# Expert weights of a routed block fetched in 4 KB pieces, with the contraction rows renumbered to match

## What is computed

```python
def hierarchical_moe(x, wg, bg, we, be, w_gate, w_up, w_down):
    ...
    g_logits = (xt @ wg + bg).astype(jnp.float32)
    ...
    e_logits = (xt @ we + be).astype(jnp.float32).reshape(-1, N_GROUPS, EXPERTS_PER_GROUP)
    ...
    for e in range(N_EXPERTS):
        h = jax.nn.silu(xt @ w_gate[e]) * (xt @ w_up[e])
        y = y + combine[:, e:e + 1] * (h @ w_down[e])
```

## Time and profile before

| What | Value |
|---|---|
| Median of 3 runs | 832.91 us (832.02 to 835.53) |
| Profiled execution, own time | 830.33 us |
| Its span | 828.3 us |
| TensorE (PE) busy | 766.8 us, 93% of the span |
| VectorE / ScalarE / GpSimd busy | 489.6 / 448.2 / 216.9 us |
| Moved by DMA | 186.75 MB |
| Chain that ended last | PE 78%, DVE 8%, ACT 5% of the span |

### The profile page before, as it was taken

How to read it: one execution, slowest core, us unless ns; L and a number is a source line. 1 busy time by engine, 2 the same in 40 slices (tenths; PEclk the granted TensorE clock), 3 DMA queues, 4 the chain that set the end, 5 groups by cost and what they waited for, 6 DMA issues and landing times.

```text
span 828.3 us, 10555 instructions
## 1 busy us (share of the span) xinstructions
PE 766.8 (93%) x3635; PEld 632.3 (76%) x3635; DVE 489.6 (59%) x639; ACT 448.2 (54%) x572; POOL 216.9 (26%) x126
## 2 busy tenths in 40 slices
PE   4999999999999999999999957999999999999960
PEld 3887878888788888888888855787888888787850
DVE  7704566576643213013122366888989898998965
ACT  6244666565733322223212315788888888888832
POOL 5555332323233444444435034000000000000013
PEclk9999999999999999999999959999999999999995
DMA  8664562521221352333348258999999999957945
GB/s 308 187 232 153 194 224 76 205 77 56 72 77 52 113 192 84 95 102 101 102 142 320 79 176 335 404 408 410 409 410 409 409 409 407 401 227 264 344 151 203
DMA packets 126631, 186.75 MB, mean 225 GB/s; under 512 B 9148, under 2 KB 61956, under 8 KB 126596
## 3 DMA queue, kind: packets, MB, share of 16 engines
q1 hardware_dynamic: 119156, 167.82, 56.2%
q10 hardware_dynamic: 5136, 10.08, 3.2%
q0 software_dynamic: 2304, 8.39, 2.8%
HBM read 158.99 MB, written 27.28 MB: 225 GB/s over the span
## 4 chain that ended last, share of the span: by engine, by line
PE 78%; DVE 8%; ACT 5%; issue 3%; POOL 2%; DMA 2%; ACTq 1%; POOLq 0%; DVEq 0%; SPq 0%
PE ps L974 24%; PE ps L976 23%; PE ps L975 23%; PE ps L1199 2%; DVE w_lo L371 1%; PE ps L1037 1%; PE ps L1063 1%; PE ps L1147 1%; ACT w_hi L360 1%; PE ps L1206 1%; DMA x<-in_x 1%; POOL slots L613 1%; PE ps L1048 1%; DMA raw_mg<-slots,slot_idx 1%; ACT xn L906 1%
## 5 line engine op out<-in xcount | busy, mean ns | idle before, releaser
L365 POOL TENSOR_TENSOR w_lo<-raw,w_hi 128x1024 fp32r<-128x1024 f32 x72 | 175.0, 2434 | 256.2 <-ACT w_hi L353 256.2
L353 ACT ACTIVATE w_hi<-raw 128x1024 fp32r<-128x1024 f32 x73 | 76.9, 1058 | 183.8 <-PE ps L976 174.1
L974 PE MATMUL ps<-xn_hi,w_hi 128*128 128x512 f32 x352 | 141.9, 403 | 0.0
L976 PE MATMUL ps<-xn_hi,w_lo 128*128 128x512 f32 x352 | 137.4, 390 | 0.0
L975 PE MATMUL ps<-xn_lo,w_hi 128*128 128x512 f32 x352 | 137.2, 390 | 0.0
L974 PE MATMUL ps<-w_hi,xT_hi 128*128 128x512 f32 x256 | 103.2, 403 | 10.8 <-DVE xT_lo L1708 5.4
L976 PE MATMUL ps<-w_hi,xT_lo 128*128 128x512 f32 x256 | 100.1, 391 | 0.0
L975 PE MATMUL ps<-w_lo,xT_hi 128*128 128x512 f32 x256 | 100.0, 390 | 0.0
L640 POOL DMA_INDIRECT raw_mg<-slots,slot_idx x7 | 6.8, 978 | 297.0 <-ACTq L957 288.7
L975 PEld LDWEIGHTS ps<-xn_lo,w_hi 128*128 128x128 f32 x352 | 66.2, 188 | 15.1 <-issue 1.9
L974 PEld LDWEIGHTS ps<-xn_hi,w_hi 128*128 128x128 f32 x352 | 66.2, 188 | 14.9 <-issue 1.9
(11 more groups left out here) (279 smaller groups left out, 1437.9 us busy)
## 6 DMA issues: line engine op xcount, KB each, us to landing
raw<-in_w_in SPq DMA_DIRECT2D x52, 512.0 KB, 3.7
raw_mg<-in_exp_w_down SPq DMA_DIRECT2D x36, 512.0 KB, 8.3
raw<-in_exp_w_gate SPq DMA_DIRECT2D x28, 512.0 KB, 9.9
raw_a<-in_exp_w_gate SPq DMA_DIRECT2D x27, 512.0 KB, 9.8
raw_c<-in_exp_w_up SPq DMA_DIRECT2D x27, 512.0 KB, 8.8
slots<-raw SPq DMA_DIRECT2D x24, 512.0 KB, 6.5
raw_mg<-in_exp_w_up SPq DMA_DIRECT2D x21, 512.0 KB, 9.2
raw<-in_exp_w_up SPq DMA_DIRECT2D x16, 512.0 KB, 9.2
```

What stands on the lines that cost most here:

```text
L353: nc.scalar.activation(w_hi[:, b % HI_SLOTS, :], raw_buf(b), ACT.Copy)\
L365: eng.tensor_tensor(w_lo[:, b % HI_SLOTS, :], raw_buf(b), w_hi[:, b % HI_SLOTS, :].bitcast(F32), ALU.subtract)\
L974: pe.matmul(dst, hi_l, hi_r, start=start, stop=False)
L976: return pe.matmul(dst, lo_l, hi_r, start=False, stop=stop)
```

## The change

It changes which bytes a block holds, and with that which rows of the contraction stand on which partition.

- **Gate and up blocks.** Row 8p + k of the weights goes to partition p, group k. A block is two neighbouring k, so each partition reads one piece of 4 KB, and neighbouring partitions' pieces start 16 KB apart.
- **Down blocks.** A block is 128 full rows of 1024 columns: one piece of 4 KB a partition, the block being one run of 512 KB. It holds one contraction group for both halves of the output, so TensorE fills three matmuls into bank 5 and three into bank 6, block after block (`down_block`).
- **Rows written in that order.** VectorE writes `xn2` permuted: column 8j + k goes to place k * 128 + j. It reads `x_rows` and `g2_rows` with a step of 8 floats (32 bytes) and writes without gaps. Everything that reads `xn2` (transposes, scatter, tile 0) is unchanged.
- **Router weights.** They are read in the same numbering. The pieces that land in SBUF stay 16 and 64 bytes.

```diff
+        def by_eighths(rows):
+
+            return rows.rearrange("p (j k) -> p k j", k=KD)
...
             def load_block(places, r, src):
                 bufs, sems = places
-                sp.dma_start(bufs[r].rearrange("p (k n) -> p k n", k=2), src).then_inc(sems[r], 16)
+                sp.dma_start(bufs[r], src).then_inc(sems[r], 16)
 
             def tile_source(e, before, r):
 
-                if r < 4:
-                    return rows2(w_g[e], 2 * r, 0)
                 if r < 8:
-                    return rows2(w_u[e], 2 * (r - 4), 0)
-                return rows2(w_d[before], 2 * (r % 2), 512 * ((r - 8) // 2))
+                    w = (w_g, w_u)[r // 4][e]
+                    return w.rearrange("(p k) n -> p (k n)", k=KD)[:, 2 * (r % 4) * DE:2 * (r % 4 + 1) * DE]
+                return w_d[before][(r - 8) * P:(r - 7) * P, :]
...
-                    act.dma_start(router_w[:, :, 0:NG], a["router_grp_w"][0].rearrange("(k p) n -> p k n", p=P))\
+                    act.dma_start(router_w[:, :, 0:NG], a["router_grp_w"][0].rearrange("(p k) n -> p k n", k=KD))\
...
-                    act.dma_start(router_w[:, :, NG:], a["router_exp_w"][0].rearrange("(k p) n -> p k n", p=P))\
+                    act.dma_start(router_w[:, :, NG:], a["router_exp_w"][0].rearrange("(p k) n -> p k n", k=KD))\
...
+            def down_block(slot, k):
+                for c in range(2):
+                    mm = three(ps[:, 5 + c, :], hT_hi[:, k, :], hT_lo[:, k, :],
+                               w_hi[:, slot, c * 512:(c + 1) * 512], w_lo[:, slot, c * 512:(c + 1) * 512],
+                               k == 0, k == DE // P - 1)
+                mm.then_inc(S["w_used"], 1)
...
                     if r < 8:
-                        expert_block(slot, r // 4, 2 * (r % 4), KD, xT_hi, xT_lo)
+                        expert_block(slot, r // 4, 2 * (r % 4))
                     else:
-                        expert_block(slot, 5 + (r - 8) // 2, 2 * (r % 2), DE // P, hT_hi, hT_lo)
+                        down_block(slot, r - 8)
...
-                dve.scalar_tensor_tensor(out=xn2[:, t, :], in0=x_rows[:, t, :], scalar=stat[:, 5, t:t + 1],
-                                         in1=g2_rows[:, :], op0=ALU.mult, op1=ALU.mult)\
+                dve.scalar_tensor_tensor(out=xn2[:, t, :].rearrange("p (k j) -> p k j", j=P),
+                                         in0=by_eighths(x_rows[:, t, :]), scalar=stat[:, 5, t:t + 1],
+                                         in1=by_eighths(g2_rows[:, :]), op0=ALU.mult, op1=ALU.mult)\
```

More of the change, by code:

```diff
@@ L534, in _ @@
                 lo_wait_loop(sp, n_last + (PAIRED - 1), r - PER_TILE)
-                load_block(EVEN, r, tile_source(last, last, 8 + r))
+                sp.dma_start(even_buf[r], tile_source(last, last, 8 + r)).then_inc(even_in[r], 16)
             for t in range(NT):
@@ L1207, in turn_h, with expert_block @@
                 mm.then_inc(S["hT_ps"], 1)
-            def expert_block(slot, bank, k0, n_k, hi, lo):
+            def expert_block(slot, bank, k0):
                 for kk in range(2):
                     k = k0 + kk
-                    mm = three(ps[:, bank, :], hi[:, k, :], lo[:, k, :],
+                    mm = three(ps[:, bank, :], xT_hi[:, k, :], xT_lo[:, k, :],
                                w_hi[:, slot, kk * 512:(kk + 1) * 512], w_lo[:, slot, kk * 512:(kk + 1) * 512],
-                               k == 0, k == n_k - 1)
+                               k == 0, k == KD - 1)
+                mm.then_inc(S["w_used"], 1)
[4 more added lines that the diff above has]
+                               k == 0, k == DE // P - 1)
                 mm.then_inc(S["w_used"], 1)
@@ L1227, in _ @@
                 lo_wait(pe, B_EXP + r)
-                expert_block(r % HI_SLOTS, r // 4, 2 * (r % 4), KD, xT_hi, xT_lo)
+                expert_block(r % HI_SLOTS, r // 4, 2 * (r % 4))
             turn_x(x_odd, S["x_odd_in"], 16)
@@ L1266, in _ @@
                 lo_wait_loop(pe, tiles, r)
-                expert_block((8 + r) % HI_SLOTS, 5 + r // 2, 2 * (r % 2), DE // P, hT_hi, hT_lo)
+                down_block((8 + r) % HI_SLOTS, r)
         @block.vector
```

## The result

| | before | changed |
|---|---|---|
| median of 7 runs | 833.36 us (829.56 to 835.83) | 838.5 us (837.64 to 839.42) |
| profiled execution, own time | 830.33 us | 838.5 us |
| its span | 828.3 us | 836.7 us |
| granted TensorE clock, mean | 0.975 | 0.968 |
| DMA packets | 126631 | 102056 |

The ratio is 1.006 with an interval of 1.004 to 1.0081: the changed kernel is 0.6% slower, 5.1 us. The forecast of 834.1 us and its range up to 837.0 do not hold it.

What follows compares the result with a forecast made beforehand. TensorE was taken to bound the expert tiles, with the DMA stream full but hidden. The terms 0 + 0 + 1.2 + 0 gave +1.2 us, 832.91 to 834.1 us for the median, range 829.6 to 837.0.

Steps and rivals of the forecast that it cites:

- Gate, up and down in 4 KB pieces: Expert tiles: transfers may get quicker, but TensorE's own work covers them; 0 us.
- The estimate of 5% more per share: SP's queue in the expert tiles: larger pieces move 5% more per share, a tile's transfers 17.1 us instead of 17.9.
- Down blocks over two banks: Expert tiles' down matmuls: same 24 matmuls, seven bank changes a tile instead of one, each costing nothing; 0 us.
- Rows written permuted: VectorE's strided reads when writing xn2: only the last of four writes is on the path; +1.2 us.
- The bound of a factor of three: High end for VectorE's xn2 write, from its slowest two-input SBUF operation, 2056 ns for 692: 2.6 us more.
- Router weights: ScalarE's two router weight transfers before the tiles: same small pieces in SBUF, so same issue time; 0 us.
- a second 0.90 us: ScalarE's issue of the larger router weight transfer: if it took another 0.90 us, the cost would be 0.4 us.
- The slower stream: Expert tiles: pieces 16 KB apart slow the DMA stream, deciding under some 365 GB/s; 852 us at 15% less; chance 6%.
- the landings: TensorE's waits for w_lo and GpSimd were really late weights; quicker transfers gain up to 5.2 us, 828.9; chance 6%.
- The first rival: Slower DMA stream in the expert tiles: 25 us spare, used up at 10% slowdown; 852 us at 15%; chance 6%.
- The third rival: Small costs add up: xn2 read at three times, late ScalarE at router weights or bank changes; about 837.5 us; chance 5%.
- A gap on TensorE near 449 us: Sign of being wrong: TensorE waiting where it uses GpSimd's last remainder at 449.13, before the expert tiles.

Runs made afterwards that it cites:

- down_4kb: Changed kernel with gate and up blocks back in 2 KB pieces, down blocks still in 4 KB pieces over two banks: 834.11 us, ratio 1.0019.
- router_last: Changed kernel with the two transfers of the router's weights issued behind the other four on ScalarE's queue: 834.67 us, ratio 1.0017.

## Why the prediction was wrong

**Gate, up and down in 4 KB pieces: 0 us.** Right for the tiles, and by the reasons given: 419 GB/s for 410, landings shorter by 1.2 us, SP's waits longer, tiles unchanged. The estimate of 5% more per share came out as 2%. But the step looked for the stream's neighbours only from 510 us on. The same transfers start at 427 us, in the middle of the router's.

**Down blocks over two banks: 0 us.** Right; `down_4kb` shows no loss that the strided write does not explain.

**Rows written permuted: +1.2 us.** Mechanism right, size somewhat high: the instruction grew by 0.9 us where 1.19 was taken, and TensorE's wait by 0.8; for the last of the four, the one on the path, it is 2.07 us for 1.28. The first of the four stayed covered. The Trainium skill's rule on 16-byte lines (SBUF — State Buffer, "SBUF: two separate sides") excluded zero, and the trace agrees, with 2.19 us for 1.285. The bound of a factor of three, borrowed from an operation of another kind, was far off.

**Router weights: "I take 0".** This is the step that failed, and it cost 4.3 of the 5.1 us. Its arithmetic held: "a delay of ScalarE beyond 0.47 us reaches TensorE", and of the 4.9 us of delay 4.3 did. The input was wrong. I asked only whether the two router transfers change, found their pieces the same, and expected the same issue time. For these two that was even right (1.35 and 0.93 us for 1.40 and 0.90), and the one delay that was priced, a second 0.90 us, did not come. The cost was in the issue behind them, which the prediction did not name: with all of the router's pieces the same in SBUF it took 2.5, 6.1 or 10.4 us, by what SP's queue had in flight. The rows on record held the hint, a pause of 9.55 us of which the transfers shown account for a tenth; I did not ask what filled it.

The mechanism is in the traces: in the same 4 us both queues move equal numbers of pieces, 783 each with pieces of 2 KB and 443 each with pieces of 4 KB, a factor of 1.8 for ScalarE's queue. The Trainium skill states a rule that fits (DMA: Bandwidth & Descriptors, "Queues, rings and completion order"): each DMA engine goes round the queues that have work for it, a packet at a time. The trace agrees with the taking of turns. The page counts several descriptors to a packet, and how many pieces make one turn the equal counts do not show. What sets how long ScalarE's own queue stops stays open: the stop ends after 789 and 886 pieces in the two kernels, which fits a limit on pieces under way, but in `router_last` it falls on the second large transfer, after 417, and no run varied it.

**The spare in the rivals.** The slower stream and the landings did not come. The first rival's arithmetic counted 19.5 us of lull as wholly free, though the engines move 110 of 404 GB/s in it; that leaves 14 us, 20 instead of 25 in all, and its turning point is at 8%, 372 GB/s. No run came near it.

**The third rival.** It let small costs add up to about 837.5 us and held the right clause ("a ScalarE late at the router's weights") at 5%, but beside two that did not happen, and priced at the wrong size. A late ScalarE should have been a rival of its own: one mechanism, its spare of 0.47 us known, its price open upward. "A gap on TensorE near 449 us" was named among the signs of being wrong, and there it is.

## What to carry to other kernels

A change of piece size in one queue is a change for every queue that runs beside it: list all transfers in flight wherever the changed ones run, small-piece ones first, and price their issuing engine's stop as open. Where an engine that computes also issues transfers of many small pieces, and has less than a microsecond in hand, issue those before the large stream starts or from a queue that can wait. And a step taken out of a DMA's pattern comes back in an engine's: 1.7 times on VectorE here, and on TensorE free only where weight loads are covered.

## What was not expected of the hardware

- The issue of a 2 KB transfer held its queue, and the engine behind it, for 2.46, 6.11 or 10.37 us: with no expert weights beside it, beside 2 KB pieces, beside 4 KB pieces. Two queues with work moved equal numbers of pieces, whatever the sizes: 782 and 783, 442 and 443.
- VectorE's 128x1024 operation with a step took 2.06 us (output alone, 512 bytes), 2.19 (both inputs, 32 bytes) and 2.26 (all three, 32 bytes): the cost does not add over operands.
- A weight load of 128 x 128 f32 with a step of 32 bytes took 336 ns for 192 in the gather at 2.4 GHz, 338 for 333 at 1.2 GHz, and 190 for 140 in the transposes.
- From about 475 to 510 us the granted clock differs between executions, with and without the change: eight transposes take 1.09 or 1.97 us, the logits 5.75 or 6.86. Differences of that size in this stretch of one profile say nothing about a change.
